# Packing the query heads of a latent-attention layer into full TensorE tiles, with their rope parts together, on one Trainium2 core

## The reference, cut to what matters

```python
c_q = rms_norm(p_cq, q_norm_g)                                   # p_cq: T x 384, from xn @ w_in
q = (c_q @ w_uq).reshape(B, T, MLA_HEADS, QK_NOPE + QK_ROPE)     # 8 heads of 64 + 32
q_nope = q[..., :QK_NOPE]
q_pe = apply_rope(q[..., QK_NOPE:], cos[:, None, :], sin[:, None, :])
k_pe = apply_rope(p_kr, cos, sin)                                # p_kr: T x 32, shared by all heads
# apply_rope: x1, x2 = halves of x;  [x1 cos - x2 sin, x1 sin + x2 cos]
# scores = q_nope . k_nope + q_pe . k_pe, causal softmax, times v
```

## Time and profile before

| | |
|---|---|
| median of 3 runs | 1181.56 us (1181.07 to 1181.73) |
| the profiled execution's own time | 1181.36 us |
| its span in the trace | 1179.6 us |
| instructions | 13314 |
| TensorE busy | 1141.4 us, 97% of the span |
| VectorE, ScalarE busy | 228.5 us, 187.3 us |
| read from memory | 440.52 MB |

### The profile page before, as it was taken

One profiled execution on the slowest core, in us unless ns is written; L12 is line 12 of the kernel. 1 busy time (PEld: TensorE's weight loads), 2 busy tenths in 40 slices (PEclk: granted clock), 3 DMA queues, 4 the chain that ended last, 5 costly groups with the idle time before them and its releaser, 6 DMA issues.

```text
span 1179.6 us, 13314 instructions
## 1 busy us (share of the span) xinstructions
PE 1141.4 (97%) x5598; PEld 530.4 (45%) x5598; DVE 228.5 (19%) x528; ACT 187.3 (16%) x404; POOL 0.2 (0%) x4
## 2 busy tenths in 40 slices
PE   9999999999999999999999999999998989898997
PEld 7767888855243333333343433333333333333332
DVE  4555621114111111111111112111111111111112
ACT  2257620002011110101010111101000001010102
POOL 0000000000000000000000000000000000000000
PEclk9999999999999999999999999999999999999999
DMA  9834434387999999999999999999999999999996
GB/s 377 348 143 179 150 119 162 146 344 290 399 422 429 428 431 432 432 431 430 434 430 432 432 432 431 430 434 430 432 432 432 431 431 433 431 431 432 426 426 272
DMA packets 26128, 442.03 MB, mean 375 GB/s; under 512 B 4144, under 2 KB 4656, under 8 KB 7408
## 3 DMA queue, kind: packets, MB, share of 16 engines
q1 hardware_dynamic: 23472, 439.19, 88.3%
q10 hardware_dynamic: 2624, 2.39, 0.6%
HBM read 440.52 MB, written 1.05 MB: 374 GB/s over the span
## 4 chain that ended last, share of the span: by engine, by line
PE 73%; DMA 25%; ACT 1%; DVE 0%; issue 0%; SPq 0%; another core or an unknown queue 0%; ACTq 0%; DVEq 0%
PE ps L880 28%; DMA work<-in_w_exp_dram 24%; PE ps L899 12%; PE ps L538 11%; PE ps L867 4%; PE ps L855 4%; PE ps L747 2%; PE ps L810 2%; PE ps L830 2%; PE ps L771 1%; PE ps L615 1%; ACT work L1297 1%; PE ps L889 1%; DMA ring<-in_w_mix_dram 1%; PE ps L581 1%; PE ps L861 1%
## 5 line engine op out<-in xcount | busy, mean ns | idle before, releaser
L880 PE MATMUL ps<-ring,work 128*64 128x512 f32 x1536 | 341.0, 595 | 12.6 <-DMA ring<-in_w_exp_dram 12.6
L880 PEld LDWEIGHTS ps<-ring,work 128*64 128x64 f32 x1536 | 109.0, 137 | 228.9 <-issue 217.6
L1733 DVE TENSOR_SCALAR work<-ps 128x512 f32<-128x512 f32 x32 | 22.1, 691 | 742.2 <-PE ps L880 742.2
L538 PE MATMUL ps<-work,ring 128*128 128x256 f32 (+2 forms) x576 | 129.5, 384 | 0.0
L880 PE MATMUL ps<-work 128*64 128x512 f32 x512 | 116.2, 596 | 5.1 <-DMA work<-in_w_exp_dram 5.1
L899 PE MATMUL ps<-ring,work 128*64 128x512 f32 x512 | 113.6, 595 | 5.5 <-ACT work L1297 3.8
L899 PE MATMUL ps<-work 128*64 128x512 f32 x512 | 114.0, 596 | 3.9 <-ACT work L1297 3.8
L538 PEld LDWEIGHTS ps<-work,ring 128*128 128x128 f32 (+1 forms) x576 | 107.1, 188 | 19.1 <-issue 1.2
L880 PEld LDWEIGHTS ps<-work 128*64 128x64 f32 x512 | 34.9, 137 | 82.1 <-issue 72.6
L899 PEld LDWEIGHTS ps<-ring,work 128*64 128x64 f32 x512 | 35.5, 137 | 73.4 <-issue 65.4
L899 PEld LDWEIGHTS ps<-work 128*64 128x64 f32 x512 | 35.2, 137 | 72.8 <-issue 62.8
(11 more groups left out here) (237 smaller groups left out, 617.3 us busy)
## 6 DMA issues: line engine op xcount, KB each, us to landing
ring<-in_w_exp_dram SPq DMA_DIRECT2D x52, 4096.0 KB, 39.9
work<-in_w_exp_dram SPq DMA_DIRECT2D x26, 4096.0 KB, 39.9
ring<-in_w_exp_dram SPq DMA_DIRECT2D x23, 2048.0 KB, 10.8
ring<-in_w_mix_dram SPq DMA_DIRECT2D x29, 1024.0 KB, 7.1
work<-in_w_exp_dram SPq DMA_DIRECT2D x10, 2048.0 KB, 12.2
work<-in_w_exp_dram SPq DMA_DIRECT2D x4, 1024.0 KB, 44.4
ring<-in_w_exp_dram SPq DMA_DIRECT2D x2, 1024.0 KB, 5.6
ring<-in_w_mix_dram SPq DMA_DIRECT2D x2, 576.0 KB, 18.2
```

The source lines that it names most:

```text
L538: ins = nc.tensor.matmul(ps[part:part + width, b, 0:hi - lo], wv[:, k, o:o + width], xnT[:, k, lo:hi], start=(k == 0), stop=(k == KT - 1))
L880: ins = nc.tensor.matmul(ps[CAP * c:CAP * c + CAP, b, :], xeT[:, k, CAP * (u % 2):CAP * (u % 2) + CAP], wu[:, k % SPAN, 512 * q:512 * q + ...
L1733: V.tensor_scalar(hg, ps[:, 0, :], LIMIT, None, ALU.min).then_inc(glu_ready, 1)
```

## The change

- The weights of `q` are reordered on the host: of each group of four heads first the four 64-wide parts, then the four rope parts of 32. A group of four heads is then three tiles of 128 channels: two with two heads' 64-wide parts each, and one with the rope parts of all four. There are six `q` jobs of three matmuls of 128 output channels x 256 tokens, in place of eight of 96.
- ScalarE reads a tile of two heads with two copies of 64 partitions (the second from partitions 64 to 127 to 0 to 63), and a rope tile with one copy of 128 partitions into `qrope`.
- The rotation of the queries is four matmuls of 32x32 weights and 512 columns, one on each quadrant (rows 32j and columns 32j), all into bank 4, after the third `k` job. The wait for `rope_ready` 1 ahead of it is gone from TensorE and stands now on VectorE.
- VectorE multiplies with sine and with cosine once each on 128 partitions x 512, and then adds four times 32x512, from partitions 32j to the partitions 64 to 95 of heads j and j + 4. Each addition counts `rope_ready`.
- `kr`: K tile k goes to column group k mod 4 (32 columns each), so a partition group holds the sum of K tiles k and k + 4. ScalarE copies all 128 partitions to `krope`. A matmul with `rotm` on 128 rows adds the four parts and rotates them (bank 6); one more with `foldm` (four stacked unit matrices) adds them without rotating (bank 7). VectorE's cosine product reads bank 7 rather than SBUF.
- The constants grow by 32 columns; `rot`, `cos` and `sin` are filled on all partitions.

```diff
+            if kind == "uq":
+                heads = m.reshape(Q_LORA, 2, HEADS // 2, QD)
+                m = np.concatenate([heads[..., :NOPE].reshape(Q_LORA, 2, -1), heads[..., NOPE:].reshape(Q_LORA, 2, -1)], axis=2)
+                m = m.reshape(Q_LORA, HEADS * QD)
...
+        qrope = view(2 * SEQ, gel_at + 4 * SEQ).rearrange("p (k t) -> p k t", k=2)
+        krope = view(T, gel_at + 2 * SEQ)
...
-        jobs += [("q", h) for h in range(HEADS)] + [("k", g) for g in range(HEADS // 2)] + [("v", i) for i in range(3)]
+        jobs += [("q", t) for t in range(6)] + [("k", g) for g in range(HEADS // 2)] + [("v", i) for i in range(3)]
...
-            project(("kr", 0), OFF_KR, ROPE, 0, T, part=NOPE, last=True)
+            n, o, w = in_cols(OFF_KR)
+            wait_load(n)
+            b = begin(("kr", 0))
+            wv = ring[:, slot_of(n), 0:KT * w].rearrange("p (k n) -> p k n", k=KT)
+            for k in range(KT):
+                q = ROPE * (k % 4)
+                ins = nc.tensor.matmul(ps[q:q + ROPE, b, 0:T], wv[:, k, o:o + ROPE], xnT[:, k, :], start=(k < 4), stop=(k >= 4))
+                if k == 0:
+                    settle(ins)
+            ins.then_inc(proj_done, 1)
+            owed[0] += 1
...
-            nc.tensor.matmul(ps[NOPE:QD, 6, 0:T], rotm, kh[NOPE:QD, 0, :], start=True, stop=True).then_inc(krot_done, 1)
+            nc.tensor.matmul(ps[NOPE:QD, 6, 0:T], rotm, krope, start=True, stop=True)
+            nc.tensor.matmul(ps[NOPE:QD, 7, 0:T], foldm, krope, start=True, stop=True).then_inc(krot_done, 1)
...
-            for h in range(HEADS):
-                n = load_at[("uq", 384 * (h // 4))]
+            for t in range(6):
+                n = load_at[("uq", 384 * (t // 3))]
...
-                    ins = nc.tensor.matmul(ps[0:QD, b, 0:SEQ], wv[:, k, QD * (h % 4):QD * (h % 4) + QD], cq[:, k, :],
+                    ins = nc.tensor.matmul(ps[:, b, 0:SEQ], wv[:, k, P * (t % 3):P * (t % 3) + P], cq[:, k, :],
...
-                if g >= 2:
-                    if g == 2:
-                        pe.wait_ge(proj_read, JOB[("q", HEADS - 1)] + 1)
-                        pe.wait_ge(rope_ready, 1)
-                        pe.wait_ge(lora_var, 2)
-                    for r in (2 * g - 4, 2 * g - 3):
-                        nc.tensor.matmul(ps[NOPE:QD, 4 + r, :].rearrange("p (h t) -> p h t", h=2), rotm,
-                                         qh[NOPE:QD, 2 * r:2 * r + 2, :], start=True, stop=True).then_inc(qrot_done, 1)
+                if g == 2:
+                    pe.wait_ge(proj_read, JOB[("q", 5)] + 1)
+                    pe.wait_ge(lora_var, 2)
+                    for j in range(4):
+                        ins = nc.tensor.matmul(ps[ROPE * j:ROPE * j + ROPE, 4, :].rearrange("p (k t) -> p k t", k=2),
+                                               rotm[ROPE * j:ROPE * j + ROPE, :], qrope[ROPE * j:ROPE * j + ROPE, :, :],
+                                               start=True, stop=True)
+                    ins.then_inc(qrot_done, 1)
...
-                    ins = nc.scalar.activation(kh[NOPE:QD, 0, :], ps[NOPE:QD, b, 0:T], ACT.Copy)
+                    ins = nc.scalar.activation(krope, ps[:, b, 0:T], ACT.Copy)
...
-                    ins = nc.scalar.activation(qh[0:QD, i, :], ps[0:QD, b, 0:SEQ], ACT.Copy)
+                    if i % 3 == 2:
+                        ins = nc.scalar.activation(qrope[:, i // 3, :], ps[:, b, 0:SEQ], ACT.Copy)
+                    else:
+                        h = 4 * (i // 3) + 2 * (i % 3)
+                        nc.scalar.activation(qh[0:NOPE, h, :], ps[0:NOPE, b, 0:SEQ], ACT.Copy)
+                        ins = nc.scalar.activation(qh[0:NOPE, h + 1, :], ps[NOPE:P, b, 0:SEQ], ACT.Copy)
...
-            link(V.tensor_tensor(kh[NOPE:QD, 0, :], kh[NOPE:QD, 0, :], cosT, ALU.mult))
+            link(V.tensor_tensor(kh[NOPE:QD, 0, :], ps[NOPE:QD, 7, 0:T], cosT, ALU.mult))
...
-            for g in range(4):
-                dve.wait_ge(qrot_done, g + 1)
-                q2 = qh[NOPE:QD, 2 * g:2 * g + 2, :]
-                V.tensor_tensor(ropeu[NOPE:QD, :, :], ps[NOPE:QD, 4 + g, :].rearrange("p (h t) -> p h t", h=2), sin2, ALU.mult)
-                link(V.tensor_tensor(q2, q2, cos2, ALU.mult))
-                ins = V.tensor_tensor(q2, q2, ropeu[NOPE:QD, :, :], ALU.add)
...
+            dve.wait_ge(qrot_done, 1)
+            dve.wait_ge(rope_ready, 1)
+            V.tensor_tensor(ropeu, ps[:, 4, :].rearrange("p (k t) -> p k t", k=2), sin2, ALU.mult)
+            link(V.tensor_tensor(qrope, qrope, cos2, ALU.mult))
+            for j in range(4):
+                V.tensor_tensor(qh[NOPE:QD, j:HEADS:4, :], qrope[ROPE * j:ROPE * j + ROPE, :, :],
+                                ropeu[ROPE * j:ROPE * j + ROPE, :, :], ALU.add).then_inc(rope_ready, 1)
```

More of the change, by code:

```diff
@@ L79 @@
 _n = 0
-for _name, _w in (("ones", 128), ("ident", 128), ("mask", 272), ("rot", 32), ("cos", T), ("sin", T), ("head", 2)):
+for _name, _w in (("ones", 128), ("ident", 128), ("mask", 272), ("rot", 32), ("cos", T), ("sin", T), ("head", 2), ("fold", 32)):
     CA[_name] = (_n, _n + _w)
@@ L104, in constants @@
         rot[r, r + half] = 1.0
-    a[NOPE:QD, slice(*CA["rot"])] = rot
+    a[:, slice(*CA["rot"])] = np.tile(rot, (P // ROPE, 1))
+    a[:, slice(*CA["fold"])] = np.tile(np.eye(ROPE, dtype=np.float32), (P // ROPE, 1))
     inv = (np.float32(ROPE_BASE) ** (-np.arange(0, ROPE, 2, dtype=np.float32) / np.float32(ROPE))).astype(np.float32)
     ang = np.arange(T, dtype=np.float32)[:, None] * inv[None, :]
-    a[NOPE:QD, slice(*CA["cos"])] = np.tile(np.cos(ang).astype(np.float32).T, (2, 1))
-    a[NOPE:QD, slice(*CA["sin"])] = np.tile(np.sin(ang).astype(np.float32).T, (2, 1))
+    a[:, slice(*CA["cos"])] = np.tile(np.cos(ang).astype(np.float32).T, (2 * P // ROPE, 1))
+    a[:, slice(*CA["sin"])] = np.tile(np.sin(ang).astype(np.float32).T, (2 * P // ROPE, 1))
     b = np.zeros((P, NCB), np.float32)
@@ L283, in layer @@
         head = ca[:, slice(*CA["head"])]
-        rotm = ca[NOPE:QD, slice(*CA["rot"])]
+        rotm = ca[:, slice(*CA["rot"])]
+        foldm = ca[:, slice(*CA["fold"])]
         cosT = ca[NOPE:QD, slice(*CA["cos"])]
@@ L608, in _ @@
             pe.wait_ge(lora_ready, 1)
-            for h in range(HEADS):
-                n = load_at[("uq", 384 * (h // 4))]
+            for t in range(6):
+                n = load_at[("uq", 384 * (t // 3))]
                 wait_load(n)
-                b = begin(("q", h))
+                b = begin(("q", t))
                 wv = ring[:, slot_of(n), 0:QT * 384].rearrange("p (k n) -> p k n", k=QT)
                 for k in range(QT):
-                    ins = nc.tensor.matmul(ps[0:QD, b, 0:SEQ], wv[:, k, QD * (h % 4):QD * (h % 4) + QD], cq[:, k, :],
+                    ins = nc.tensor.matmul(ps[:, b, 0:SEQ], wv[:, k, P * (t % 3):P * (t % 3) + P], cq[:, k, :],
                                            start=(k == 0), stop=(k == QT - 1))
@@ L619, in _ @@
                 ins.then_inc(proj_done, 1)
-                if h % 4 == 3:
+                if t % 3 == 2:
                     owed[0] += 1
@@ L1507, in _ @@
             gelu_arg_of(0)
-            cos2 = ca[NOPE:QD, CA["cos"][0] + N_META:CA["cos"][1]].rearrange("p (a t) -> p a t", a=1).broadcast_to([ROPE, 2, SEQ])
-            sin2 = ca[NOPE:QD, CA["sin"][0] + N_META:CA["sin"][1]].rearrange("p (a t) -> p a t", a=1).broadcast_to([ROPE, 2, SEQ])
-            for g in range(4):
-                dve.wait_ge(qrot_done, g + 1)
-                q2 = qh[NOPE:QD, 2 * g:2 * g + 2, :]
-                V.tensor_tensor(ropeu[NOPE:QD, :, :], ps[NOPE:QD, 4 + g, :].rearrange("p (h t) -> p h t", h=2), sin2, ALU.mult)
-                link(V.tensor_tensor(q2, q2, cos2, ALU.mult))
-                ins = V.tensor_tensor(q2, q2, ropeu[NOPE:QD, :, :], ALU.add)
-                if g < 3:
-                    ins.then_inc(rope_ready, 1)
-                    dve.wait_ge(rope_ready, g + 2)
-                else:
-                    ins.then_inc(rope_ready, 1)
+            cos2 = ca[:, CA["cos"][0] + N_META:CA["cos"][1]].rearrange("p (a t) -> p a t", a=1).broadcast_to([P, 2, SEQ])
+            sin2 = ca[:, CA["sin"][0] + N_META:CA["sin"][1]].rearrange("p (a t) -> p a t", a=1).broadcast_to([P, 2, SEQ])
+            dve.wait_ge(qrot_done, 1)
[5 more added lines that the diff above has]
+                                ropeu[ROPE * j:ROPE * j + ROPE, :, :], ALU.add).then_inc(rope_ready, 1)
             def gelu_end(p):
```

## The result

The changed kernel takes 1171.95 us (median of 4 runs, 1171.89 to 1173.82) against 1181.48 for the kernel before; the ratio is 0.9923, 95% interval 0.9911 to 0.9936. Run again, unaltered, it gave 1172.79 (ratio 0.9927, 0.9914 to 0.9941), 8.7 us. The forecast had the sign and most of the size, and missed a term of about 2 us.

What follows compares the result with a forecast made beforehand. The prediction took the expert-load stream to set the end and TensorE's mixer its start. Its terms, -2.70 + 0.46 - 2.59 - 2.64 = -7.47 us, took the median of 1181.56 to 1174.1 us, range 1172.8 to 1177.5.

Steps and rivals of the forecast that it cites:

- What bounds the kernel: Whole kernel: expert loads set the end, TensorE's mixer their start; a microsecond off TensorE before 240 us saves one.
- The rival that nothing reaches the end: End of the kernel: mixer releases don't start the full stream, so the last transfer lands as now; 1181.5, chance 0.05.
- Parts 1 to 4: TensorE in the mixer: kr -2.70 us, keys' rotation +0.46, q -2.59, queries' rotation -2.64.
- that rival: kr: only two column groups run at a time, 1.93 us, total 1175.1; chance 0.08 shared with no overlap in kr.
- The rotation in one bank: Queries' rotation: four matmuls sharing a bank overlap, 1.02 us for 3.66; rival in series, 1176.7, chance 0.08.
- Waits that might have come back: Beside TensorE: ScalarE, VectorE and SyncE cause it no new wait; the GeLU argument keeps 1.5 us of slack.
- A sign of being wrong: Profile after the change: a clock row under 1.00, among the listed signs that the forecast was wrong.
- the rival that named it: TensorE's clock falls to 1.2 GHz at the new forms (28 and 57 us); 1189 if lasting 30 us, chance 0.04.
- What lies beside: Work off TensorE's path: VectorE, ScalarE and SyncE stay covered, and the wider constants get no term.
- The range: Total time: 1172.8 to 1177.5 us, from cheaper rounds, a form switch and spread below, one overlap missing above.

Runs made afterwards that it cites:

- e4: The changed kernel with 16 more matmuls of 272 columns into an unused bank ahead of the q jobs: 1180.96 us.
- e12: The changed kernel with the rope part of the keys (kr) as before and no fold, constants still wide: 1174.96 us.
- e2_before_pad: The kernel before with only the constants' tensor in memory 32 columns wider, zeros that are not transferred: 1181.25 us, ratio 0.9996.
- e5: The kernel before with an unused on-chip tensor of 32 columns between the constants and vec, small and work: 1179.45 us.
- e7: The changed kernel with the fold matrix in a tensor of its own behind work, brought by its own transfer: 1174.60 us.
- e8: The changed kernel with the fold matrix in a tensor of its own directly behind the constants, ahead of vec: 1172.10 us.
- e9: The kernel before with an unused gap of 9 columns (36 bytes) ahead of vec, small and work: 1181.51 us.
- e10: The changed kernel with the fold matrix in its own tensor behind the constants, plus a gap of 41 columns ahead of vec: 1173.84 us.
- e15: The kernel before with 32 unused columns ahead of the ring and 32 more ahead of work, aligning only the ring: 1178.54 us.
- e13: The kernel before with 32 unused columns ahead of the ring, putting ring and work both on a multiple of 256 bytes: 1178.37 us.

## Why the prediction was right, and where it was wrong

- **What bounds the kernel** (the stream of loads to the end, its start set by TensorE's mixer): right. e4 gives 8.2 us for 7.3 (7.0 in the traces) and e12 2.2 to 3.0 for 2.2. The rival that nothing reaches the end is out.
- **Parts 1 to 4**: right within 0.1 us each, -7.53 us in all against -7.47. kr's two rounds on four groups cost 1.05 us against the 0.97 taken from the k job's pairs; two groups would have cost 1.96, so that rival's price (1.93) was right and its case wrong.
- **The rotation in one bank**: no cost. 0.99 us in one bank, 0.99 in four. By the rule of the Trainium skill that the prediction weighed ("TensorEngine Tiling (Array Packing)", section "Gotcha 1: PSUM Pressure") the quadrants would have had to follow one another; for row tiles that also differ in their column tiles, these runs don't show it.
- **Waits that might have come back**: none did. ScalarE loads the table for the tanh at 57.05 us, 1.6 us after the GeLU argument was ready at 55.44 (forecast 1.5; its own figures, 17.9 less 16.2, give 1.7).
- **A sign of being wrong** that did come: granted clock under 1.00, 0.99 over the last stretch. It isn't the rival that named it. It fell late in the stream, not at the new forms at 28 and 57 us, where the chain's pieces kept their full-clock lengths, and e2_before_pad, without the change, has 0.97 from 990 to 1090 us.
- **What failed** is the sentence that closes "What lies beside": "no load is added or moved; ca grows by 16 KB beside loads of 1 MB". It took the wider constants for a transfer alone and gave them no term. They also move work on chip by 128 bytes a partition, and so the destination of a third of the expert loads onto a multiple of 256 bytes. In a kernel whose last 880 us run at the rate of its DMA engines that is worth 2.1 us (e5), 2.5 by e7 against e8. Against it stands a start that was 0.60 us later in the trace. Together, -7.5, +0.3 to 0.6 and -2.1 to -2.5 make 9.0 to 9.7 us below 1181.5; the two medians lie at 9.5 and 8.7. The two terms that the prediction lacked have opposite signs and partly cancel. Without the side effect (e7) the forecast of 1174.1 met 1174.60.
- **The range** was built from TensorE's terms alone. Its low end had no row for the stream's rate, on which the longest stretch of the kernel hangs. Its sums are also off: the terms that it names give 1173.3 below (it has 1173.0) and 1177.1 above (it has 1177.5), which changes nothing in where the result fell.

That the place of the loads' destination on chip is what counts is shown. That it counts modulo 256 rests on twelve kernels at three values (0, 128, 192). With the ring at 128, a start of work at 0 was always faster, and 192 was as 128 within the noise (e9 against before; e10 and e7, 1173.84 and 1174.60, with ranges that overlap). By the same addresses each fast start is 256 modulo 512, so 0 modulo 512 is untested, as is 64 modulo 256. And a tensor that moves is also read by the engines at its new place; no run tells a slower write from a write that meets those reads. The Trainium skill describes a cost of starts off a multiple of 256 bytes in "DMA: Bandwidth & Descriptors", section "How a descriptor splits into AXI transactions": a descriptor that doesn't start on 256 bytes has its first transaction start at the boundary below, and the bytes before it still cost. It says so of reads; here the destination moved, so the page bears on this only if writes are split the same way, which no run here shows apart. A packet of 32 KB, taken as one descriptor 128 bytes past a multiple, would by that page take 129 transactions for 128, by estimate 1028 beats for 1024, 0.4%. The packets here went from 1217.3 to 1213.9 ns, 0.3%. That the parts don't add up, the page doesn't say.

## What to carry to other kernels

Where TensorE is gapless up to the point from which the loads run without a pause, a microsecond of it is worth a microsecond at the end, even if the end is set by the loads: add up the pieces in the chain of waits. Here four small matmuls on column groups or quadrants of their own cost little more than one (0.99 us for four of 512 columns, where one after the other they took 3.66), also in a shared bank; take the price from rows with the same arrangement. And a tensor that grows moves all that is allocated behind it: in a kernel bound by its loads, look at where their destinations start, try an unused gap ahead of them, and credit what an unused gap gives to the gap and not to the change.

## What the runs showed of the hardware beyond that

- Placing the ring's rows on a multiple of 256 bytes took the 32 KB packets of a full stream to 1213 ns almost without exception: 3.1 us over the kernel with the ring alone (e15), 3.3 by a single unused tensor ahead of it (e13).
- Additions on VectorE that read partitions 0 to 31, 32 to 63 or 96 to 127 and write 64 to 95 took 0.7 us each for 32x512, as the one that reads and writes 64 to 95 (2.83 us for the four).
- In the changed kernel's trace the granted clock was 0.98 over each of two stretches of 100 us in the stream and 1.00 in the one before them. TensorE waited for loads in these stretches, but it did so as much in the same stretches of the kernel before, whose clock stayed at 1.00; what made it fall is open. The stream set the pace there, and its rate was the same:

```profile
783.00:883.00 100.00, 97.49 (x490) 36.59 (x484) 11.79 (x27) 10.58 (x23) 0.00 (x0) 1.00 1.00 433
883.00:983.00 100.00, 94.04 (x452) 34.40 (x449) 12.38 (x25) 9.02 (x19) 0.00 (x0) 0.98 1.00 432
983.00:1083.00 100.00, 93.67 (x458) 34.81 (x459) 12.36 (x28) 10.46 (x22) 0.00 (x0) 0.98 1.00 433
```
